# The experts of a two-layer encoder trunk in full fp32 on four column tiles, with a ring of seven weight slots, in place of split fp32r products

## The reference

```python
logits = (xt @ router_w).astype(jnp.float32)
top_logit, top_idx = lax.top_k(logits, TOP_K)          # TOP_K = 2, N_EXPERTS = 8
gate = jax.nn.softmax(top_logit, axis=-1)
...
def expert_block(args):
    xblk, e = args
    return (jax.nn.silu(xblk @ w_gate[e]) * (xblk @ w_up[e])) @ w_down[e]
...
out = jnp.zeros((t + 1, d), jnp.float32).at[slot_tok].add(yb.astype(jnp.float32) * slot_w[:, None])
```

## Time and profile before

| | us |
|---|---|
| median of 3 runs | 1498.85 (1498.6 to 1501.92) |
| span of the profiled execution | 1499.8 |
| TensorE busy | 1464.1 (98%) |
| VectorE busy | 1130.0 (75%) |
| ScalarE busy | 910.1 (61%) |
| from the first to the last expert matmul | 530.3 to 1488.6, 958.3 |

### The profile page before, as it was taken

How to read it: one execution, slowest core, us unless ns; L and a number is a source line. 1 busy time by engine, 2 the same in 40 slices (tenths; PEclk the granted TensorE clock), 3 DMA queues, 4 the chain that set the end, 5 groups by cost and what they waited for, 6 DMA issues and landing times.

```text
span 1499.8 us, 22808 instructions
## 1 busy us (share of the span) xinstructions
PE 1464.1 (98%) x9048; PEld 1228.9 (82%) x9048; DVE 1130.0 (75%) x1073; ACT 910.1 (61%) x875; POOL 100.7 (7%) x68
## 2 busy tenths in 40 slices
PE   6999999999999999999999999999999999999997
PEld 6998859999987578888888888888888888888885
DVE  5765445544454498998888898898988899889786
ACT  5631234443455266776776777777776777777674
POOL 4330010000000000000000000000000000000000
PEclk9999999999999999999999999999999999999999
DMA  7531127555533479999999999999999999999993
GB/s 275 207 116 58 59 67 237 168 185 185 211 128 133 149 272 390 376 374 387 363 367 366 389 390 380 388 374 372 391 376 360 375 388 365 394 377 376 377 387 123
DMA packets 194144, 436.96 MB, mean 291 GB/s; under 512 B 5320, under 2 KB 28160, under 8 KB 193968
## 3 DMA queue, kind: packets, MB, share of 16 engines
q1 hardware_dynamic: 189248, 423.64, 77.0%
q0 software_dynamic: 2832, 9.26, 2.4%
q10 hardware_dynamic: 2016, 3.38, 0.7%
HBM read 428.38 MB, written 7.88 MB: 291 GB/s over the span
## 4 chain that ended last, share of the span: by engine, by line
PE 73%; DMA 10%; DVE 9%; ACT 5%; issue 3%; POOL 1%; DVEq 0%; SPq 0%; ACTq 0%
PE bank L1579 20%; PE bank L1580 20%; PE bank L1581 20%; DVE weights_lo L1209 4%; DMA weights<-in_moe_w_gate 4%; DMA weights<-in_moe_w_up 4%; DMA weights<-in_moe_w_down 2%; PE bank L2005 2%; PE bank L1805 2%; ACT weights_hi L762 2%; DVE ws L1022 2%; PE bank L1615 1%; PE bank L2129 1%; ACT qkv_hi L641 1%; PE bank L1720 1%
## 5 line engine op out<-in xcount | busy, mean ns | idle before, releaser
L1209 DVE TENSOR_TENSOR weights_lo<-weights,weights_hi 128x2048 fp32r<-128x2048 f32 (+1 forms) x396 | 823.0, 2121 | 149.3 <-ACT weights_hi L762 147.8
L762 ACT ACTIVATE weights_hi<-weights 128x2048 fp32r<-128x2048 f32 (+1 forms) x396 | 685.4, 1781 | 274.7 <-DMA weights<-in_moe_w_up 99.7
L1579 PE MATMUL bank<-weights_hi,expert_x_hi 128*128 128x512 f32 x896 | 354.9, 396 | 1.9 <-DVE expert_x_lo L1447 1.0
L1581 PE MATMUL bank<-weights_hi,expert_x_lo 128*128 128x512 f32 x896 | 349.4, 390 | 0.0
L1580 PE MATMUL bank<-weights_lo,expert_x_hi 128*128 128x512 f32 x896 | 349.2, 390 | 0.0
L1579 PE MATMUL bank<-weights_hi,hidden_hi 128*128 128x512 f32 x520 | 204.5, 393 | 3.1 <-DVE hidden_lo L1247 3.1
L1580 PE MATMUL bank<-weights_lo,hidden_hi 128*128 128x512 f32 x520 | 202.6, 390 | 0.0
L1581 PE MATMUL bank<-weights_hi,hidden_lo 128*128 128x512 f32 x520 | 202.6, 390 | 0.0
L1581 PEld LDWEIGHTS bank<-weights_hi,expert_x_lo 128*128 128x128 f32 x896 | 168.3, 188 | 36.4
L1579 PEld LDWEIGHTS bank<-weights_hi,expert_x_hi 128*128 128x128 f32 x896 | 168.3, 188 | 36.3 <-DVE expert_x_lo L1447 1.4
L1580 PEld LDWEIGHTS bank<-weights_lo,expert_x_hi 128*128 128x128 f32 x896 | 168.4, 188 | 33.3
(11 more groups left out here) (338 smaller groups left out, 1593.6 us busy)
## 6 DMA issues: line engine op xcount, KB each, us to landing
weights<-in_moe_w_down SPq DMA_DIRECT2D x56, 2048.0 KB, 9.6
weights<-in_moe_w_up SPq DMA_DIRECT2D x56, 2048.0 KB, 9.5
weights<-in_moe_w_gate SPq DMA_DIRECT2D x55, 2048.0 KB, 9.8
weights<-in_a_w_in SPq DMA_DIRECT2D x7, 2048.0 KB, 8.7
weights<-in_ffn_w_up SPq DMA_DIRECT2D x11, 1024.0 KB, 5.2
weights<-in_ffn_w_gate SPq DMA_DIRECT2D x11, 1024.0 KB, 5.4
weights<-in_ffn_w_down SPq DMA_DIRECT2D x11, 1024.0 KB, 4.9
weights<-in_a_w_out SPq DMA_DIRECT2D x2, 2048.0 KB, 8.0
```

The costliest lines, as they stand in the source:

```text
L762: act.activation(hi[:, j * n:(j + 1) * n], slot[k][:, j * n:(j + 1) * n], ACT.Copy).then_inc(w_hi[k], 1)
L1209: dve.tensor_tensor(to[:, c], slot[k][:, c], hi[:, c].bitcast(F32), ALU.subtract).then_inc(w_lo[k], 1)
L1579: pe.matmul(dst, ah, bh, start=start, stop=False, skip_group_check=True)
L1581: return pe.matmul(dst, al, bh, start=False, stop=stop, skip_group_check=True)
```

## The change

- **Lanes and tiles.** `BLOCK` is 96: three lanes of 32 tokens. A matmul has 32 tokens stationary (one lane, one k-tile) and writes 32 rows of PSUM, that is one of four column tiles of the array. Four such matmuls stand side by side: in `e_up` (L2151) up columns 0 to 511, up 512 to 1023, gate 0 to 511 and gate 512 to 1023 on tiles 0 to 3 of bank `b`, for lanes b = 0, 1, 2. Down (`e_down`, L2195) puts four blocks of 256 output columns side by side.
- **Full fp32.** The weights are used as loaded: `product`, `w_round` and `w_rest` are gone from the experts, ScalarE and VectorE do only silu, product, copies.
- **Three and a half steps.** An item has three steps of 1024 hidden columns and one of 512. Up per step 96 fp32 matmuls of 512 columns (the last: 96 of 256), down 28 k-tiles x 3 lanes x 4 blocks = 336 of 256 columns.
- **Ring.** Seven slots of 2 MB (`ring0` to `ring6`) instead of three; 21 loads per item in the order of use. Gate and up chunks are 512 rows of 1024 columns.
- **Turning.** The hidden tile is 64 rows by 512 columns per lane; `e_turn` (L2181) makes 12 transposes of 64 columns per step (6 in the last).
- **Rows.** The result lies in quarters of 256 columns, so `ye` has three parts and GpSimd adds it with three indirect DMAs of 128 quarter rows each (L616). The first down projection of an item now waits for `m_free`, the landing of all three from the item before. `slots` has eight small matmuls instead of two; `OVER` is 5 instead of 3, so the chain of small VectorE operations that counts the items is longer.
- **Spares.** All 17 are gone. In the last item the scatter (L2135) is 24 matmuls on row tiles of 32, after all down projections.

```diff
-BLOCK = 128
+LANE = 32
+BLOCK = 3 * LANE
+WIDE = 2 * 512
 OVER = TOPK * T // (BLOCK + 1)
+RING = 7
...
+            e_load(6, r4[6], e_in(mg, 0, 0, 0), s_qmm, 4)
+            e_load(0, r4[0], e_in(mu, 0, 0, 0), s_qmm, 4)
+            e_load(1, r4[1], e_in(mg, 0, 0, 1), s_qmm, 4)
+            e_load(2, r4[2], e_in(mu, 0, 0, 1), s_aw, 3)
+            e_load(4, r4[4], e_in(mg, 0, 1, 0), s_aw, 4)
+            e_load(5, r4[5], e_in(mu, 0, 1, 0), s_aw, 4)
...
+                for b in range(3):
+                    pool.indirect_dma_start(out=h_quarters[:, :],
+                                            out_offset=bass.IndirectOffsetOnAxis(ap=quarter_row[1][:, b:b + 1], axis=0),
+                                            in_=ye[:, b, :], in_offset=None, compute_op=ALU.add).then_inc(m_added, 16)
+                pool.wait_ge(m_added, i * 48 + 48)
                 pool.sem_inc(m_free, 1)
...
+            def e_up(i, at, s, first=False):
+                for hf in range(2):
+                    (kg, ng), (ku, nu) = in_ring(i, at + 2 * hf), in_ring(i, at + 2 * hf + 1)
+                    pe.wait_ge(ring_in[kg], ng)
+                    pe.wait_ge(ring_in[ku], nu)
+                    for kt in range(4):
+                        for b in range(3):
...
+                            for g in range(4):
+                                w = r4[(ku, kg)[g // 2]]
+                                m = pe.matmul(bank[b][LANE * g:LANE * g + LANE, :],
+                                              xe[:, 4 * hf + kt, LANE * b:LANE * b + LANE],
+                                              w[:, kt, (g % 2) * 512:(g % 2) * 512 + 512],
...
+            def item(i, last):
+                s0 = i * 4
+                e_turn(s0)
+                e_up(i, 0, s0 + 1)
+                pe.wait_ge(m_free, i + 1)
+                e_down(i, 4, s0, start=True)
+                e_turn(s0 + 1)
...
+                    slots(i + 1)
+                e_up(i, 6, s0 + 2)
+                e_down(i, 10, s0 + 1)
+                e_turn(s0 + 2)
...
+                e_up_last(i, 12, s0 + 3)
+                if not last:
+                    turn_rows(i)
+                e_down(i, 14, s0 + 2)
...
+                e_turn(s0 + 3, 2)
+                if not last:
+                    e_up(i, 16, s0 + 4)
+                e_down(i, 20, s0 + 3, stop=True)
```

More of the change, by code:

```diff
@@ L215, in trunk @@
         g8 = [view(s, 0, KT, 512) for s in slot]
[L216 removed]
+        r4 = [view(s, 0, 4, WIDE) for s in ring]
+        r8 = [view(s, 0, KT, 512) for s in ring]
         kq = ws[:, 0:4096].rearrange("p (a j n c) -> p a j n c", a=2, j=JP, n=NC)
@@ L1480, in e_pass @@
-                rests(moe, s0 + (NE - 1), between=None if last else lambda: gathered(i + 1), more=not last,
-                      down=not last, last=last)
-                if not last:
-                    rests(moe, s0 + NE, extra=lambda: out_half(i))
+                e_hidden(s0 + 2)
+                e_turned(s0 + 2)
+                e_hidden(s0 + 3, 256)
+                if not last:
+                    gathered(i + 1)
+                e_turned(s0 + 3, 2)
+                if not last:
+                    e_hidden(s0 + 4)
@@ L1485, in _ @@
+                item_out(i, last)
             gathered(0)
-            slots(0)
             link(dve.tensor_copy(cnt, bank[3][:, 0:8]))
-            link(dve.tensor_scalar(over, cnt, float(BLOCK), None, ALU.is_gt))
+            for k in range(2):
+                link(dve.tensor_scalar(over[:, k * E:(k + 1) * E], cnt, float((k + 1) * BLOCK), None, ALU.is_gt))
             link(dve.tensor_reduce(nover, over, AX.X, ALU.add))
-            for k in range(1, 8):
+            for k in range(1, 2 * E):
@@ L1926, in _ @@
                       start=True, stop=True).then_inc(s_kmm, 1)
-            def spare(n):
-                wh = view(whi[0], 0, KT, 512)
-                for _ in range(n):
-                    pe.matmul(bank[2][:, :], wh[:, 0, 0:P], wh[:, 0, :], start=True, stop=True)
             def query(g):
@@ new lines, in scatter @@
+            def scatter(i):
+                pe.wait_ge(m_X, i * 2 + 4)
+                pe.wait_ge(m_y, i * 3 + 3)
+                for t in range(NT):
+                    for b in range(3):
+                        for q in range(4):
+                            r = slice(LANE * q, LANE * q + LANE)
+                            m = pe.matmul(bank[scatter_at[t][q]][:, 0:256], PT[r, b, t * P:(t + 1) * P], ye[r, b, :],
+                                          start=b == 0, stop=b == 2)
+                            if b == 2:
+                                m.then_inc(m_sc, 1)
@@ L2191, in _ @@
+                if not last:
+                    e_up(i, 16, s0 + 4)
+                e_down(i, 20, s0 + 3, stop=True)
             pe.wait_ge(m_P, 2)
             first_gather()
+            pe.wait_ge(m_X, 2)
+            e_up(0, -5, 0, first=True)
             slots(0)
-            spare(6)
-            e_proj(0, 0, m_g, rows=m_Xl)
-            e_proj(1, 0, m_u)
             pe.wait_ge(s_items, 1)
@@ L2199, in _ @@
             with pe.Fori(0, n_more) as i:
-                e_pass(i, False)
-            e_pass(n_more, True)
-            for half_ in range(2):
-                scatter(n_more, half_)
+                item(i, False)
+            item(n_more, True)
+            scatter(n_more)
 def kernel(**inputs):
```

523 lines of the change are left out of this document (252 added, 271 removed).

## The result

The changed kernel takes 1508.85 us (median of four runs; 1508.16 to 2366.6) where the kernel before takes 1499.32 (four runs beside it). The ratio is 1.0061, 95% interval 1.0045 to 1.0077: 0.6% slower, where 1.1% faster was forecast; it lies inside the range, but on the side that had the chance of 0.30. The profiled execution took 1508.99 us, with a span of 1506.9. Three single runs lie far outside (here 2366.6 us at a mean granted clock of 0.59, in e6 7023.72 us at 1.00, in e10 1514.14 us at 0.94); the ratios leave them out, and their cause was not found.

The account below looks back on a forecast made before the run. TensorE was taken as the bound, the DMA 3% behind. Experts from 527.1 plus 937.3 end at 1464.4; loop code 4.9 and tail 14.5 give a span of 1483.8, forecast 1483 us, range 1456 to 1530.

Parts of the forecast that it names:

- gap at the loop's turn: Sign of a wrong forecast: TensorE pausing where its item loop turns; code loading was put at 0.7 us a turn.
- start of the experts: Before the first up projection: gather from 521.35 taking 5.1 us, then copies of 0.6, so experts begin at 527.1.
- items and rows, no jump: TensorE's expert work: eight items' passes, transposes and mode changes 917.6, rows and slots 16.1, with small terms 937.3 us.
- tail behind the last down projection: After the last matmul: copies, scatter and eight additions add 3.3 to the old 11.2, 14.5 us; ends 11.2 and 20.
- Four tiles give four: Up and down projections: four column tiles overlap by factor four, 0.1075 us a wide pass, 108.4 us an item.
- The rival: Projections: four tiles give less than four; 867 us more if they gave what two give; chance 0.14, slower.
- Transposes: Turning of the hidden tile: 42 per item at 0.11 us each, 4.6 us; 2.3 if the weight load hides.
- Changes between the modes: TensorE switching tile modes: 11 per item at 0.155 us each, 1.7 us; ends 0.6 and 4.4.
- The prediction's rival: Weight loads: DMA becomes the bound from 5.5 us a load, 1493 to 1508; chance 0.06, half no change, half slower.
- signs named for a wrong forecast: Passes over 0.109; TensorE waiting for `m_free` or DMA; GB/s below 370; clock below 1.00 after 530; loop-turn gaps.
- The adding DMAs: Ahead of an item's first down projection: 19.4 us hidden under 22.2; rival without overlap 34 us, +83, chance 0.05.
- The counting chain: Before the held-back loads: 77 small operations instead of 41, ending at 543.4, hidden by the first up projection until 547.7.

Follow-up runs that it names:

- e6: Changed kernel with a hint for the jump of TensorE's item loop; 1489.23 us, ratio 0.9925.
- e10: Changed kernel with the loop's head at the start of a code block and the jump hint together; 1476.5 us, ratio 0.9846.
- e8: e5 with `slots` moved one place earlier, behind the item's first up projection; 1461.44 us, ratio 0.9753.
- e5: Changed kernel with TensorE's first six items written out and a loop for what is left, so no jump back; 1467.34 us, ratio 0.9791.
- e4: Items written out, one column tile's three lanes behind each other instead of the four tiles in turn, against e5; 1691.86 us.
- e2: Changed kernel, loop kept, with only half of the k-tiles of every projection; 1409.9 us.
- e1: Changed kernel with all eight items of TensorE written out and no loop; 1466.98 us, ratio 0.9779.
- e7: Changed kernel with one item written out, then two items in each loop turn, so two jumps back; 1481.5 us.

## Why the prediction was wrong

The step that failed is in the sum: "The loop's body is now written out in full (672 fp32 matmuls); whether its code stays on the core between turns no row shows; I add 0.7 a turn, 4.9, ends 0 and 3 a turn." It does not stay. A jump back costs the gap of 4.8 to 5.1 us, 0.56 more for the transposes at the lower clock (1.52 - 0.96) and 2.5 more for the up projection (23.15 - 20.63), together 7.9 us, six times 47.4. The price was outside its own ends, because they held a short pause and no clock. The mechanism was named, as a "gap at the loop's turn", and given 3 us a turn at the most, 21 us over the seven turns that the sum counts; only six of them jump back. The trace of the kernel before could have warned: its branch takes 0.21 us with 5 packets of code over all the experts, and the body grew from a loop inside the item to 672 matmuls in a row.

The account of the span from the first wide pass on, with e8 as the kernel without jumps:

| stretch or term | predicted us | measured us |
|---|---|---|
| start of the experts | 527.1 | 527.3 |
| items and rows, no jump | 937.3 | 920.5 (e8, 527.09 to 1447.62) |
| jumps back | 4.9 | 47.2 (967.7 - 920.5) |
| tail behind the last down projection | 14.5 | 11.9 (1495.0 to 1506.9) |
| span | 1483.8 | 1506.9 |

Against e5, which differs from the changed kernel by the jumps alone, the span is 42.3 longer; e5 has the four short falls of 1.7 us that the changed kernel has not, so both ways give about 8 us a jump.

The start came out right by luck. The gather began at 520.03, 1.3 us before the forecast's 521.35, and took 6.58 us instead of 5.1, at a granted clock of 0.50 in 521 to 524; the two misses cancel.

The rest went better than forecast. By item, 114.9 to 115.0 against 117.0:

- **Four tiles give four.** A wide pass starts every (20.81 - 0.59)/191 = 0.1059 us against 0.1075, a narrow one every (10.54 - 0.38)/191 = 0.0532 against 0.0538: 107.0 an item for 108.4. The rival fell for this order of the instructions. The figure of 3.07 of the Trainium skill ("TensorE: Matmul & The Clock Gate", Measured speedup vs the span model) is for four row tiles; these four column tiles do better than that. e4, at 0.152, a factor of 2.8, shows how much the order over the tiles is worth.
- **Transposes** of 64 columns start every (0.96 - 0.22)/11 = 0.067 us, not 0.11: 2.8 for 4.6. Most of the cost laid to the weight load does not show.
- **Changes between the modes** cost more: 0.26 from a narrow pass to a transpose, 0.09 from there to a wide pass, 0.29 from a wide pass to a narrow one, which had been left out. That is 2.5 an item for 1.7. Slots took 1.77 for 1.4, rows 0.81 for 0.9.
- **DMA.** Its own pace is 109.2 us an item (e2), below the lower end of 110.8. (The prediction's rival has +25 us at 5.7 us a load; its own terms give 38.) It was no bound: 368 GB/s in the changed kernel from 700 to 1100 and 395 in e8 are TensorE's pace. Of the signs named for a wrong forecast three were met, all by the jumps: "GB/s below 370", "a granted clock below 1.00 after 530" and the gaps themselves.
- **The adding DMAs** did not serialize. In the view of L616, changed kernel, before:

```profile
L616 POOL DMA_INDIRECT h_rows<-ws,quarter_row x21: 1542/1547/1636, 666.9 to 1407.6; - x21
...
DMA to landing us min/median/max: 7.0/8.0/9.2
```

  1.55 us each for 128 quarter rows, where 128 whole rows took 3.55, and TensorE never waited for `m_free`.
- **The counting chain** ended at 542.7 for 543.4, as laid out by the count of its operations.
- **Tail.** 11.9 for 14.5. The scatter overlapped on its row tiles (48 passes in 2.87 us) and the additions took 3.23 us in a row, where two pairs and a wait took 3.65 before. The differences that the prediction names add up to 2.3 us and not to its 3.3.

So the direction turned on one term: without jumps the kernel is 2.2% faster than before (e1, e5). The nearness of 1483 to 1508.85 is partly luck, since the other terms were too high: the items without jumps by 16.8 us, and with the jumps at 7.9 each the same arithmetic would have given a span of 1526.

## What to carry to other kernels

A loop is free only while its body's code stays on the core. Count the instructions of a body that is written out, and look at the duration of the closing branch in the engine's sequencer: 0.2 us with the code on the core and 6 without it, in these kernels. Where the trip count is known but for a rare case, write the usual items out and leave the loop for the rest; a written-out stretch fetched the same code with no cost that shows. A short pause is also dearer than it looks where the clock falls behind it: here 4.8 us of idle time cost 7.9. Here it also paid to keep small matmuls apart from each other (e8, 6 us), and to deal instructions round the column tiles in turn (e4, 225 us).

## What the runs showed of the hardware that was not expected

- The jump's price does not grow with the body's length: about 8 us with 14 blocks a turn, and the same in the one run with a body twice as long (e7).
- Behind two kinds of small matmuls side by side, 2.7 us without a wait, the clock fell to 1.2 GHz in four of the seven items (e1, e5); with 10 us of down projection between them it did not fall once (e8).
- With a hint, and the loop's head at a block's start, the branch that jumps falls from 6.0 to 0.36 us, and a gap of 5.0 us appears where the loop is left (e10).
- A core's DMA moved 411 GB/s over 400 us (e2), above the 379 of the earlier trace rows.
